# Dilated-attention heads scored as a band of near keys and four residue classes instead of all eight key tiles

## The reference

```python
DIL_PATTERNS = ((128, 1), (512, 4), (2048, 16))
for window, dilation in DIL_PATTERNS:
    o, l = dilated_window_attention(q, k, v, rel_bias, window, dilation)
...
wts = jax.nn.softmax(jnp.stack(lses, axis=0), axis=0)
out = jnp.einsum('pbsh,pbshd->bshd', wts, jnp.stack(outs, axis=0).astype(jnp.float32))
```

## Time and profile before

| | |
|---|---|
| median of 3 runs | 3556.41 us (3551.28 to 3556.53) |
| profiled execution, its own time | 3552.48 us |
| its span, first to last instruction | 3550.7 us |
| mean granted TensorE clock | 0.992 of full speed |
| busy PE / PEld / DVE / ACT / POOL | 97% / 81% / 58% / 48% / 47% of the span |
| DMA | 292.81 MB, 27.0% of 16 engines |
| attention, first to last score product | 323 to about 765 us, and 2077 to about 2517 us |

### The profile page before, as it was taken

How to read it: one execution, slowest core, us unless ns; L and a number is a source line. 1 busy time by engine, 2 the same in 40 slices (tenths; PEclk the granted TensorE clock), 3 DMA queues, 4 the chain that set the end, 5 groups by cost and what they waited for, 6 DMA issues and landing times. The chain is left out here.

```text
span 3550.7 us, 47741 instructions
## 1 busy us (share of the span) xinstructions
PE 3451.8 (97%) x17305; PEld 2858.6 (81%) x17305; DVE 2068.9 (58%) x3148; ACT 1715.8 (48%) x2973; POOL 1659.0 (47%) x1239
## 2 busy tenths in 40 slices
PE   8999999999899999999999999999998999999998
PEld 7788777778788888888777887777787888888886
DVE  4234888964745555455651358799366455554555
ACT  4343888974444434411353358789553344343113
POOL 1133554443477676423342435534345776763223
PEclk9999999999999999999999999999999999999999
DMA  5442320122122121422324413211232121213213
GB/s 181 128 104 75 77 75 23 42 84 96 53 68 78 58 78 58 144 80 82 118 70 135 127 52 90 57 34 32 75 107 67 62 78 59 78 58 137 95 66 119
DMA packets 247439, 292.81 MB, mean 82 GB/s; under 512 B 43244, under 2 KB 197182, under 8 KB 247167
## 3 DMA queue, kind: packets, MB, share of 16 engines
q1 hardware_dynamic: 247207, 289.76, 27.0%
HBM read 202.70 MB, written 80.31 MB: 80 GB/s over the span
## 5 line engine op out<-in xcount | busy, mean ns | idle before, releaser
L1709 DVE TENSOR_TENSOR pl<-ps,ph 128x512 fp32r<-128x512 f32 (+1 forms) x576 | 376.4, 654 | 66.4 <-ACT ps L1540 65.9
L1432 PE MATMUL ps<-q,k 97*128 97x512 f32 (+4 forms) x1296 | 387.1, 390 | 17.2 <-DVE pl L1709 7.0
L3098 DVE TENSOR_TENSOR y<-ps,y 128x512 f32<-128x512 f32 (+1 forms) x432 | 260.2, 602 | 230.8 <-PE ps L291 227.7
L1539 ACT ACTIVATE ph<-ps 128x512 fp32r<-128x512 f32 (+1 forms) x576 | 329.2, 572 | 135.2 <-PE ps L1432 130.6
L1540 ACT ACTIVATE ps<-ps 128x512 f32<-128x512 f32 (+1 forms) x576 | 328.4, 570 | 0.0
L1432 PEld LDWEIGHTS ps<-q,k 97*128 97x128 f32 (+2 forms) x1296 | 234.4, 189 | 86.3 <-DVE pl L1709 24.5
L1670 DVE TENSOR_REDUCE mx<-ps 128x1 f32<-128x512 f32 x352 | 242.0, 688 | 40.6 <-PE ps L1461 32.5
L1444 PE MATMUL ps<-ph,vh 128*128 128x512 f32 (+1 forms) x576 | 227.4, 395 | 0.0
L1445 PE MATMUL ps<-ph,vl 128*66 128x512 f32 (+1 forms) x576 | 219.7, 381 | 0.0
L1447 PE MATMUL ps<-pl,vh 128*128 128x512 f32 (+1 forms) x576 | 219.7, 381 | 0.0
L289 PE MATMUL ps<-hh,wh 128*128 128x512 f32 (+1 forms) x528 | 200.5, 380 | 10.1 <-PEq L283 6.2
(11 more groups left out here) (396 smaller groups left out, 10193.9 us busy)
## 6 DMA issues: line engine op xcount, KB each, us to landing
activations<-c_gate SPq DMA_DIRECT2D x44, 640.0 KB, 3.8
act_in<-activations SPq DMA_DIRECT2D x20, 1280.0 KB, 5.7
raw<-in_w_up SPq DMA_DIRECT2D x48, 512.0 KB, 4.9
up_raw<-in_w_up SPq DMA_DIRECT2D x40, 512.0 KB, 4.7
raw<-in_w_down SPq DMA_DIRECT2D x40, 512.0 KB, 3.5
heads<-stage SPq DMA_DIRECT2D x28, 640.0 KB, 3.5
rq<-heads SPq DMA_DIRECT2D x56, 320.0 KB, 4.0
raw<-in_w_in SPq DMA_DIRECT2D x32, 512.0 KB, 4.4
```

What stands on the lines that cost most here:

```text
L1432: mm = pe.matmul(out, a, b, start=(k == 0), stop=(k == len(prods) - 1))
L1539: act.activation(c.ph[g % RING][:, 0:w], scores, ACT.Exp, scale=STEP_SCALE[kind(h)]).then_inc(exp_done, 1)
L1709: dve.tensor_tensor(c.pl[g % RING][:, 0:w], bank(c, ST + g % 3, w), c.ph[g % RING][:, 0:w].bitcast(F32), ALU.subtract).then_inc(p_low, 1)
L3098: dve.tensor_tensor(y, bank(c, down_bank(it, u), w), y, ALU.add).then_inc(down_added, 1)
```

## The change

A group B head now takes 10 steps (`SPLIT_STEPS`) instead of 18:

- steps 0 and 1: the sample block, as before (256 queries, two key tiles);
- steps 2 to 5 (`class_step`): one per residue class. The queries are kept in the order of their class (four runs of 256), the keys are picked with a stride of 4. A step scores the 128 keys of the class in each half of the prompt against the 256 queries of the class. The values come from a second copy of the head's values, loaded in class order (`vh_class`, `vl_class`), in pieces of 128 queries, since the outputs of two halves lie in two banks;
- steps 6 to 9 (`near_step`): two key tiles each, against the queries at most 64 away: 192 or 256 of them.

The table of the head is in three parts, each with its own mask: near distances, same-class distances, and the sample's plain table; `th` and `tl` are their high and low parts, and an unsplit `dense` table of slope 4 serves the maxima. The maxima are still 18 products per head over all keys, now two per step: those of head 4 at steps 12 to 17 of head 3, those of heads 5 to 7 at steps 2 to 9 of the head before and at step 0 of the head itself, 14 of head 8's at steps 3 to 9 of head 7. The high parts of the values of heads 5 to 8 move from DVE to ACT, and so do those of the class copy. The table loads are split: `load_dense` for the head after next, `load_parts` for the next head, behind `move_row` of the third row. The first phase of the program writes a second line of biases to memory (`s_parts`), its class part thinned out by POOL.

```diff
-    STEPS = []
-    for half in range(2):
-        block = [(2 * half, 512 * half, 512, kt, kt == 0, kt == 7) for kt in range(8)]
-        STEPS += block[0:4] + [(1, 1024, 256, 8 + half, half == 0, half == 1)] + block[4:8]
...
+    def class_step(r):
+        tiles, values = [], []
+        for u, half in enumerate((1, 0)):
+            tiles.append((slice(512 * half + r, 512 * half + 512, 4), 256 * r, CLASSES + P * u, 256 * u, 256, 0))
+            for q in range(2):
+                values.append(("class", 4 * half + r, 2 * q, P * r, 256 * u + P * q, P, 0, u == 0 and r == 0))
+        return tiles, values, {0: [0], 2: [2]}.get(r, []), []
+    def near_step(kts, ends):
+        tiles, values, off = [], [], 0
+        for kt in kts:
+            qa, qb = max(0, kt * P - REACH), min(1024, kt * P + P + REACH)
+            each = (qb - qa) // 4
+            tiles.append((slice(kt * P, kt * P + P), qa // 4, NEAR + (qa - (kt * P - REACH)) // 4, off, qb - qa, each))
+            for q in range(2):
+                a, b = max(qa, 512 * q), min(qb, 512 * q + 512)
+                if a < b:
+                    values.append(("keys", kt, 2 * q, (a - 512 * q) // 4, off + (a - qa) // 4, (b - a) // 4, each, False))
+            off += qb - qa
+        return tiles, values, [], ends
...
+    SPLIT_STEPS = [plain_step(1, 1024, 256, 8, True, False), plain_step(1, 1024, 256, 9, False, True)]
+    SPLIT_STEPS += [class_step(r) for r in range(4)]
+    SPLIT_STEPS += [near_step((0, 7), []), near_step((1, 2), []), near_step((3, 4), [0]), near_step((5, 6), [2])]
...
+        elif kind(h) == "B":
+            for j in range(16):
+                put(h - 1, 2 + j // 2, "max", h, j)
+            put(h - 1, 7, "row", h, 0)
+            put(h - 1, 8, "row", h, 1)
+            for j in range(16, NM):
+                put(h, 0, "max", h, j)
+            put(h, 2, "row", h, 2)
...
+                for h in range(HEADS - 2):
+                    if kind(h) == "B":
+                        move_row(h, 2)
+                    if kind(h + 1) == "B":
+                        load_parts(h + 1)
+                    if kind(h + 2) == "B" and kind(h) == "B":
+                        load_dense(h + 2)
+                    if new_kv(h + 2):
+                        load_k(h + 2)
...
+                    for *item, first in parts:
+                        part(*item, first, ph, False)
+                    for *item, first in parts:
+                        part(*item, first, ph, True)
+                    pe.wait_ge(p_low, g + 1)
+                    for *item, first in parts:
+                        mm = part(*item, False, pl, False, item[2] in ends)
+                    mm.then_inc(pv_done, 1)
...
+                    split = h < HEADS and kind(h) == "B"
+                    if split and i == 4:
+                        high_values(h + 1)
+                    if i == (6 if split else 11) and h < HEADS and kind(h + 1) == "B":
+                        high_class_values(h + 1)
```

426 lines of the change are left out of this document (300 added, 126 removed).

## The result

The changed kernel takes **3565.4 us**, the median of 20 runs (3552.2 to 3580.7); the kernel before took 3555.6 in 20 runs beside them (3550.0 to 3556.9). The ratio is 1.0031, 95% interval [1.0023, 1.0040]: slower by 0.3%, just outside what a measurement tells from no change. The prediction was 3490, faster by 1.8%, with 3526 as its upper end. It was wrong by 75 us. The profiled execution took 3562.1 us.

What follows compares the result with a forecast made beforehand. PE's column count was taken as the bound. A head: 21.1 + 0.8 + 0.7 + 1.5 = 24.1 us; in all 3552.5 - 68.2 + 2 = 3486, and with the runs' median 3.9 above the profiled execution, 3490 us; range 3462 to 3526.

Steps and rivals of the forecast that it cites:

- The clock stays full: Whole kernel: TensorE's clock was to remain at full speed after the change, with no time charged for half clock.
- PE's work: Per group B head: PE's products sum to 21.1 us, for 31.6 before; 0.8 unexplained was added separately.
- narrow products: Value products under 256 columns: 0.115 us with 128 weight columns, 0.06 for a 128-column one with 66.
- Term (a): Third row, turned at step 2, needed at step 4: PE waits 0.7 us a head, range zero to 2.0.
- Term (b): Step 2's class values wait for DVE's scaling, delayed through the table's DMA and ACT's reciprocal: 1.5 us, range 0 to 4.
- the 2.2 us a head I had allowed: Waits in a group B head: 0.7 us for the third row and 1.5 for the outputs.
- Head 8: Has one maximum less: 0.2 us shorter per layer.
- Head 3: Takes over six maxima of head 4: 1.4 us on PE plus 0.6 for DVE, 2 us longer.
- The rest of the kernel: First phase: small DMAs and POOL's thinning start the residual's stores some 3 us later; 2 us charged, of 0 to 5.
- The second: Rival: in-order queues bind, heads at 26.9 us, 3512 in all; sign: heads at 27 or more, DVE over 90% busy; chance 0.22.
- The third: Rival: a narrow product costs as much as a wide one, 9.7 us more a head, 3568 in all; chance 0.07.
- The first: Rival: narrow products run at their share of columns, heads at about 22 us, 3473 in all; chance 0.15.

Runs made afterwards that it cites:

- e11: e10 with head 8 beginning with its two sample steps and head 7's row turned a step earlier; 3513.5 us.
- e14: e13 with class steps on 128 contiguous keys (the wrong ones) instead of every fourth; 3522.7 us.
- e1: Changed kernel with class steps on 128 contiguous keys (the wrong ones) instead of every fourth; 3564.4 us.
- e2: Changed kernel with the third row of heads 5 to 7 turned at step 1 instead of step 2; 3552.5 us.
- e3: Changed kernel with SP loading the next head's table parts ahead of the third row's move; 3566.1 us.
- e5: Changed kernel with DVE, in head 4, scaling head 3's outputs at the head of its step; 3549.6 us.
- e13: e11 with the outputs of heads 4 to 6 one step earlier, scaled behind the step's maxima; 3514.2 us.
- e10: e6 with PE turning the rows of the maxima in heads 3 to 7 behind the step's value products; 3518.5 us.
- e6: Changed kernel with the edits of e5 and e2 together; 3533.2 us.
- e9: e6 with class steps on 128 contiguous keys (the wrong ones), as in e1; 3553.5 us.

## Why the prediction was wrong, point by point

Summed against the profiled execution's own time, 3562.1 stands 76 us above the 3486 of the sum.

- **"The clock stays full"** was one sentence, and the largest error. Heads 4 to 7 spent 23.9 us at half clock in layer 0 and 34.1 in layer 1. At half the speed that is 58.0 / 2 = 29 us. The step had no row behind it: the earlier trace rows shows the clock full in a stream without stalls, and the change brought stalls. No bound was kept for it: the range would have had to.
- **PE's work.** The narrow products, on which I spent most, were right (0.117 and 0.060 for 0.115 and 0.06). The 16 products a head with every fourth key as weights were taken at 0.117 as the other 256-column ones: that is 1.9 us a head too little, 15 in all. With it PE's work is 21.1 + 0.8 + 1.9 = 23.8 us, and e11's head 5 is 24.9 long with 1.1 of wait: the sum closes. It is work, though, and not yet time: with contiguous keys at full clock a head got shorter by only 0.4 us (head 5 of e14) to 1.0 us (head 7 of e1), since waits grew by the rest.
- **Term (a), the third row.** The wait for its DMA, put at 0.7 a head, is there only in head 7, with 0.38. A side bank was the wait instead: the maximum two places on needs the bank that ACT had not yet copied, 1.6 us in heads 5 and 6 (e2 removed it). I had looked at who needs the row, and not at who needs its bank.
- **Term (b), the outputs.** The wait was there, on the product I named, with 1.0 to 1.2 us in heads 5 and 6, 0.5 in head 7 and 2.83 in head 4 against 1.5. The mechanism was wrong: the table's DMA does make ACT idle for 1.1 to 1.7 us, but with that gone nothing changed (e3); in head 4 DVE's order decided (e5), and in heads 5 and 6 taking the reciprocals and the scaling a step earlier brought the wait to 0.3 us or less (e13). For head 4 I had not seen that head 3's outputs fall under the other rule of DVE's program.
- **The turned rows**, 0.4 to 1.0 us twice a head, weren't in the sum at all. With one maximum a step there was a step between a maximum and the row in its bank; with two a step there is none. e10 removed them.
- What the waits of (a), (b) and the rows cost beyond the 2.2 us a head I had allowed is the rest of heads 4 to 7: 57 - 29 - 15 = 13 us, 1.6 a head. It is a remainder; counted by itself, PE's idle time in these eight stretches is 28.2 us where 17.6 were allowed, 10.6 more.
- **Head 8** was put at 0.2 us less and came out 3.9 and 4.1 longer. 2.67 us is the wait of its first values for head 7's outputs, which now end within the last two steps of that head; 1.7 is the half clock behind it (3.4 / 2). With the 0.2 a layer this is some 8.4 us that no term covered. **Head 3** was right within 0.6 us.
- **Heads 9 to 15** take 2.7 and 2.8 us more, and the sum had them unchanged. 1.4 us of it in each layer is a new wait of maxima for ACT's copy of a row. Before, PE turned a head's third row behind the step's maximum; the changed program sorts the side work by head (`side_work`, L1397), so the row comes ahead of the next head's maximum, and the maximum of the next step needs the row's bank:

```profile
651.32 0.27 PE L1648 MATMUL ps<-ident,m 128*4 128x128 f32 x1
651.35 0.49 PE L1640 MATMUL ps<-k,q 128*128 128x512 f32 x1
...
653.98 0.50 PE L1640 MATMUL ps<-k,q 128*128 128x512 f32 x1 [0.98 <-ACT row_part L1705]
```

No run put this order back, so its worth is read and not tested; another 0.3 us is more waiting for a low part, and the last 1.0 stays open.
- **The rest of the kernel** was put at 2 us more and took 7.5 more. In the two traces the half clock outside heads 3 to 8 is 73.8 and 60.4 us; half of the difference, 6.7 us, would be most of it. In the 15 traces with the change that figure goes from 58 to 81 us with nearly the same instructions, so this part is scatter as far as is known. Cut alike in both traces, the 76 us are 55 in heads 4 to 7 (57 against the forecast's own 94.4), 1 in head 3, 8 in head 8, 5.5 in heads 9 to 15 and 5.5 in the rest.
- **The rivals.** The second, in-order queues as the bound, is the right kind of cause: its 26.9 us a head fits e6's 25.8 to 27.6 well. Its sign, DVE over 90% busy, did not come (22.3 of 27.6 us in head 5 of e6): what bound was the order, not the load, of the queues. It lacked the clock. The third had the measured time, 3568, for a reason that is plainly not so: that it came near is chance. The first is excluded by the spacing of the narrow products.

In short: heads 4 to 7 were to take 94.4 us a layer and took 120.7 and 125.3. Of the 57 us between, 29 are half clock, 15 PE's work for strided loads and 13 waits beyond those allowed. The step that failed is "The clock stays full"; the waits of the new order made it fail.

## What to carry to other kernels

When PE is full and a change cuts its columns by a third, price the waits first: list for each bank and buffer who must free it, in the new order of each in-order engine, at the distance in steps that is left. A new stall of 1 to 3 us can cost several times its length, because the clock can fall with it, so a saving on PE counts only once the stalls are gone: here three changes of order, with PE's instructions and their sizes untouched, took 3565 to 3518, 1.1% below the kernel before, while faster loads gave nothing (e1) or cost 8.5 and 20 us (e14, e9). Look at the order of the side work in the heads that you don't mean to touch, too: here half of what they lost was the wait behind a row that had changed places with a maximum. A layout that helps the products (every fourth key) is paid for wherever another engine reads or writes it with that stride.

## What the runs showed of the hardware

- A 128-column float32r weight load from elements four apart took 310 ns against 188 to 190 in the changed kernel, and two 256-column products behind such loads 0.47 us against 0.24 in e9, which loads them side by side.
- 128-column float32r products start 0.117 us apart with 128 weight columns and 0.060 with 66, and 256-column ones with 128 weight columns 0.117 too: at 128 columns the load sets the pace, not the columns that stream.
- With a stride of four on one side (POOL's input, DVE's output), POOL's cast of 128x512 took 1237 ns for 610, its subtraction of 64x512 1740 for 1276, and DVE's scaling of 64x512 1076 for 678. The Trainium skill's page "GPSIMD Engine Reference" (section 7, "Performance pitfalls for Q7 kernels") puts half as much again on reads more than 8 bytes apart; the subtraction lies below that and the cast, at twice, above it.
- TensorE's granted clock fell to 0.50, its lower level, in stalls of 1.0 to 3.3 us or within 2.3 us behind them, and stayed there for 3.4 to 20.5 us; how often, the table above tells.
